# A hybrid attention, convolution, Fourier and linear-attention layer on one core: the second projection pass formed by seven half products a pair of tiles

## The reference

```python
hN = rms_norm(x, norm_g_l) * (1.0 + scale) + shift
p = hN @ w_in_l                       # 1024 -> 3616 columns
(qA, kA, vA, gA, bB, cB, hB, gB, uC, gC, qD, kD, vD, gD, aF, aB) = split_in(p)
yA = from_heads(attn_fn(q, k, v)) * silu(gA)      # window 8 x 16 plus 512 context keys
yB = short_conv(bB, cB, hB, conv_l) * silu(gB)    # bB * conv3(cB * hB)
yC = fourier_mix(uC) * silu(gC)                   # real part of a 2-D DFT, 4 groups of 64
yD = gla_mixer(...) * silu(gD)
y = concatenate([yA, yB, yC, yD]) @ w_out_l
return x + gate * y
```

## Time and profile before

| | |
|---|---|
| median of 3 runs | 2613.84 us (2611.82 to 2617.17) |
| the profiled execution | 2597.12 us, span 2595.4 us |
| TensorE busy | 2433.3 us, 94% of the span |
| VectorE, ScalarE, GpSimd busy | 1258.5, 931.3, 695.8 us |
| second projection pass | from about 944 to 1561 us |
| attention and scan | 1561 to 2168 us |

### The profile page before, as it was taken

The page is one execution under the profiler, slowest core; times in us unless marked ns, Lnnn a source line. Parts: engine busy times, 40 slices in busy tenths (PEclk is TensorE's granted clock), DMA queues, the critical chain, the costliest instruction groups (busy, mean ns, idle before and its releaser), DMA issues. The chain is left out here.

```text
span 2595.4 us, 52554 instructions
## 1 busy us (share of the span) xinstructions
PE 2433.3 (94%) x18684; PEld 1982.4 (76%) x18684; DVE 1258.5 (48%) x2614; ACT 931.3 (36%) x1954; POOL 695.8 (27%) x1014
## 2 busy tenths in 40 slices
PE   3899999999999969999999997999999995999999
PEld 1688888888888857888888876777777774888887
DVE  2534444344443434332333324667677665666665
ACT  1445454444545432111111114555556553111110
POOL 2232332323333220000000003433333333444442
PEclk8899999999999979999999998999999998999999
DMA  7655555656555452212222327877677787666663
GB/s 286 158 124 123 124 116 128 120 122 130 117 128 114 101 162 85 66 59 66 69 67 64 114 71 161 182 174 166 154 168 166 191 238 236 220 204 220 204 221 133
DMA packets 282000, 373.13 MB, mean 144 GB/s; under 512 B 52805, under 2 KB 211589, under 8 KB 280187
## 3 DMA queue, kind: packets, MB, share of 16 engines
q1 hardware_dynamic: 271660, 350.39, 52.7%
q10 hardware_dynamic: 9599, 19.75, 2.3%
q0 software_dynamic: 592, 0.99, 0.1%
HBM read 249.36 MB, written 121.66 MB: 143 GB/s over the span
## 5 line engine op out<-in xcount | busy, mean ns | idle before, releaser
L271 PE MATMUL p_ps_m<-p_w_hi,p_h_hi 128*128 128x512 f32 x1904 | 757.9, 398 | 17.0 <-DVE p_h_lo L1041 8.8
L273 PE MATMUL p_ps_m<-p_w_hi,p_h_lo 128*128 128x512 f32 x1904 | 745.5, 392 | 0.0
L272 PE MATMUL p_ps_m<-p_w_lo,p_h_hi 128*128 128x512 f32 x1904 | 744.5, 391 | 0.0
L271 PEld LDWEIGHTS p_ps_m<-p_w_hi,p_h_hi 128*128 128x128 f32 x1904 | 359.8, 189 | 94.5 <-issue 18.5
L273 PEld LDWEIGHTS p_ps_m<-p_w_hi,p_h_lo 128*128 128x128 f32 x1904 | 359.4, 189 | 77.6
L272 PEld LDWEIGHTS p_ps_m<-p_w_lo,p_h_hi 128*128 128x128 f32 x1904 | 359.9, 189 | 71.1
L1125 DVE TENSOR_TENSOR p_rows<-p_ps_m,p_silu_g 128x256 f32<-128x256 f32 x34 | 14.4, 425 | 319.8 <-ACT p_silu_g L869 319.8
L721 POOL TENSOR_TENSOR p_la<-p_la,p_cum 128x512 f32<-128x512 f32 x34 | 43.9, 1291 | 398.1 <-ACT p_cum L759 398.1
L1827 DVE COPY l_p_t<-a_ps_t 128x512 f32<-128x512 f32 (+1 forms) x136 | 91.5, 673 | 113.3 <-PE a_ps_t L1641 113.2
L703 POOL TENSOR_TENSOR q_hi_t<-q_hi,p_ones 128x128 fp32r<-128x128 f32 x2 | 0.9, 456 | 522.5 <-DMA q_lo<-s_qk_lo 522.5
L1677 PEld LDWEIGHTS a_ps_o<-a_v_win,l_p_t 128*64 128x64 f32 x2112 | 74.7, 139 | 61.9 <-issue 45.4
(11 more groups left out here) (291 smaller groups left out, 4559.5 us busy)
## 6 DMA issues: line engine op xcount, KB each, us to landing
s_scan<-b_w_raw SPq DMA_DIRECT2D x136, 128.0 KB, 2.4
a_scan<-s_scan SPq DMA_DIRECT2D x67, 258.0 KB, 6.3
a_kv<-s_kv SPq DMA_DIRECT2D x67, 256.0 KB, 6.3
a_v_win<-s_p SPq DMA_DIRECT2D x132, 128.0 KB
b_xr<-in_x_sample SPq DMA_DIRECT2D x32, 512.0 KB, 6.2
b_xt<-in_x_sample_t SPq DMA_DIRECT2D x32, 512.0 KB, 7.1
p_xt<-in_x_columns_t SPq DMA_DIRECT2D x32, 512.0 KB, 10.5
o_x<-in_x_sample SPq DMA_DIRECT2D x32, 512.0 KB, 4.7
```

What stands on the lines that cost most here:

```text
L271: pe.matmul(out, left_hi(k), right_hi(k), start=(k == 0), stop=False)
L272: pe.matmul(out, left_hi(k), right_lo(k), start=False, stop=False)
L273: last = pe.matmul(out, left_lo(k), right_hi(k), start=False, stop=(k == K8 - 1))
```

## The change

The second pass gets a function of its own, `column_stage`. Tiles go in pairs (17). The first two pairs (`PLAIN`) are made as before. In the others group 2 is still made for each tile, but groups 0 and 1 of both tiles, as a product of a 2 x 2 block matrix (tiles x depth halves) with a 2 x 2 block matrix (depth halves x column groups), are formed by Winograd's form of Strassen's scheme: seven half products of 12 matmuls (p1 to p7) in place of eight. For it sums of weights (`fold` on VectorE in the plain tiles, `fold_last` on GpSimd) and sums of x blocks (`sum_pair` on GpSimd, split by `high_sums` and VectorE) are made; the seven results are joined by ScalarE, VectorE and GpSimd through `part_a`, `part_b`, `part_c`, and GpSimd multiplies the gates (`mix_rows`). The rows of both tiles are sent at the end of a pair, the odd one first.

The space for this is taken from the early loads: only queries and keys are still loaded in the second pass. Bias table 0, context keys and their halves, context values, state and the order of the first queries move to the start of the attention stage, g and dft_whole (for the last Fourier rows) too. Fourier rows have four slots in place of three, the output stage has its own y_hi and y_lo, and waits for the convolution's taps before its first tile.

```diff
+def column_pairs(eng):
...
+def column_stage(nc, io, keep, early):
+
+    pieces = weight_pieces(PASS_BLOCKS[1])
+    pieces[:4] = [(None, 0, 0, 0, 0, 0)] * 2 + [(k, 4, GC, W_GRP, W_GRP, 0) for k in (0, 4)]
...
+            def send_rows(t, s, p):
...
+                else:
+                    sp.wait_ge(gates_done, t + 1)
+                    sp.wait_ge(mixed[s], p + 1)
+                gates = rows[s][:, 1:3, :].rearrange("t a c -> t (a c)")
...
+                else:
+                    columns = lambda a: a.rearrange("(a b) c -> b a c", b=GRID_W)[bass.ds(2 * t, 2)]
+                    sp.dma_start(columns(io["conv_u"][SKIP[0]:SKIP[0] + N_GRID, :]), rows[s][:, 0, :]).then_inc(rows_sent[s], 16)
+                    sp.dma_start(columns(io["gates_bc"][0:N_GRID, :]), gates).then_inc(rows_sent[s], 16)
...
+                for s in range(2):
+                    t = p * 2 + s
+                    if prompt(p):
+                        continue
+                    sp.wait_ge(lo_done if plain(p) else s_lo_done, t + 1)
+                    load_turned(t + 2, s, kind(t + 2))
+                    load_norm(t + 2, s, kind(t + 2))
...
+                    sp.wait_ge(s_lo_done, 2 * PAIRS)
+                    for to, name in (("q_hi", "qk_hi"), ("q_lo", "qk_lo")):
+                        sp.dma_start(early[to][:, :, :].bitcast(F32), io[name][0:2, :, queries].rearrange("p k t -> k p t")).then_inc(early_in, 16)
...
+                else:
+                    send_columns(p * 2, 0)
+                send_rows(p * 2 + 1, 1, p)
+                send_rows(p * 2, 0, p)
...
+            def fold_last(k):
+
+                for n, (a, b, op) in enumerate(((w_hi[:, K4 + k, 512:1024], w_lo[:, K4 + k, 512:1024], ALU.add), (part_c, w_hi[:, k, 512:1024], ALU.subtract),
+                                                (part_c, w_lo[:, k, 512:1024], ALU.subtract))):
...
+            def sum_pair(p):
+                pool.wait_ge(lo_done, p * 2 + 2)
+                a11, a12, a21, a22 = xt[0][:, 0:K4, :], xt[0][:, K4:K8, :], xt[1][:, 0:K4, :], xt[1][:, K4:K8, :]
+                pool.tensor_tensor(a22, a21, a22, ALU.add).then_inc(summed, 1)
+                pool.tensor_tensor(a21, a11, a21, ALU.subtract).then_inc(summed, 1)
+                pool.wait_ge(summed, p * 4 + 2)
+                pool.tensor_tensor(a11, a22, a11, ALU.subtract).then_inc(summed, 1)
+                pool.wait_ge(summed, p * 4 + 3)
+                pool.tensor_tensor(a12, a12, a11, ALU.subtract).then_inc(summed, 1)
+
+            def mix_rows(p, s, part, done):
+                pool.wait_ge(group_kept, p * 2 + 1 + s)
+                pool.wait_ge(done, p + 1)
+                pool.tensor_tensor(rows[s][:, 1, :], rows[s][:, 1, :], part[:, 0:W_GRP], ALU.mult)
+                pool.tensor_tensor(rows[s][:, 0, :], rows[s][:, 0, :], part[:, W_GRP:512], ALU.mult).then_inc(mixed[s], 1)
+
+            pool.wait_ge(t_lo_done, 3 * K4)
+            pool.wait_ge(plain_mm, 3 * 2 * PLAIN - 2)
+            for k in range(2):
+                fold_last(k)
+            for p in column_pairs(pool):
...
+                    continue
+                sum_pair(p)
+                if isinstance(p, int) and p == PLAIN:
+                    for k in range(2, K4):
+                        fold_last(k)
+                pool.wait_ge(u3_done, p + 1)
+                pool.wait_ge(a5_kept, p + 1)
+                pool.tensor_tensor(part_a, part_a, part_b, ALU.add).then_inc(u4_done, 1)
+                pool.tensor_tensor(part_b, part_c, part_b, ALU.add).then_inc(c22_done, 1)
+                mix_rows(p, 1, part_b, c22_done)
+                mix_rows(p, 0, part_a, c12_done)
...
+            def high_sums(p, s):
...
+            def keep_group(p, s, done):
+                act.wait_ge(rows_sent[s], p * 32 + 16)
+                act.activation(rows[s][:, 0, :], bank_b[s][:, 0:W_GRP], ACT.Copy)
+                act.activation(rows[s][:, 1, :], bank_b[s][:, W_GRP:512], ACT.Silu).then_inc(done, 1)
...
+            for t in range(2 * PLAIN):
...
+                act.wait_ge(plain_mm, plain_at(t, 0))
+                if t > 1:
+                    act.wait_ge(y_mm, t - 1)
+                act.activation(g_sb[s], plain_bank[s][0][:, 0:W_GRP], ACT.Copy)
+                act.wait_ge(rows_sent[s], p * 32 + 16)
+                act.activation(rows[s][:, 2, :], plain_bank[s][0][:, W_GRP:512], ACT.Silu).then_inc(plain_g, 1)
+                if t:
+                    act.wait_ge(plain_mm, 3 * t)
+                high(t + 1, 1 - s)
+                act.wait_ge(t_sums, 7 * t + 7)
+                for n, part in enumerate((part_a, part_b, part_c)):
+                    last = act.activation(t_hi[:, n, t, :], part, ACT.Copy)
+                last.then_inc(t_hi_done, 1)
+                if t:
...
+            for p in column_pairs(act):
+                if plain(p):
+                    continue
+                for s in range(2):
...
+                keep_group(p, 0, group_kept)
+                keep_columns(p * 2 - 1, 1, p - 1)
+                act.wait_ge(group_mm, p * 2 + 2)
+                keep_group(p, 1, group_kept)
+                if isinstance(p, int) and p == PLAIN:
+                    act.wait_ge(t_lo_done, 3 * K4)
+                act.wait_ge(mixed[0], p)
+                act.wait_ge(p1_mm, p + 1)
+                act.activation(part_a, bank_x[:, :], ACT.Copy).then_inc(a1_kept, 1)
+                act.wait_ge(c11_done, p + 1)
+                act.activation(rows[0][:, 2, :], rows[0][:, 2, :], ACT.Silu).then_inc(gates_done, 1)
+                act.wait_ge(mixed[1], p)
+                act.wait_ge(p5_mm, p + 1)
...
+                    act.wait_ge(p4_mm, p + 1)
+                    high(p * 2 + 3, 1)
+                act.wait_ge(c21_done, p + 1)
...
+            def half_product(out, left, right):
...
+                for k in range(K4):
+                    pe.matmul(out, left(0, k), right(0, k), start=(k == 0), stop=False)
+                    pe.matmul(out, left(0, k), right(1, k), start=False, stop=False)
+                    last = pe.matmul(out, left(1, k), right(0, k), start=False, stop=(k == K4 - 1))
+                return last
...
+                for s in range(2):
+                    pe.wait_ge(lo_done, p * 2 + 1 + s)
...
+                pe.wait_ge(a5_kept, p)
...
+                    pe.wait_ge(plain_rows, 2 * PLAIN - 1)
...
+                if begin:
...
+                pe.wait_ge(s_lo_done, p * 2 + 2)
...
+                    pe.wait_ge(plain_g, 2 * PLAIN)
+                half_product(bank_z[:, :], lambda part, k: sums[part][0][:, k, :], lambda part, k: turned[part][:, 1, k, :]).then_inc(p6_mm, 1)
+                pe.wait_ge(a1_kept, p + 1)
+                half_product(bank_x[:, :], lambda part, k: sums[part][1][:, K4 + k, :], lambda part, k: turned[part][:, 0, k, :]).then_inc(p5_mm, 1)
...
+                    first_step(p * 2, 0, g_done)
+                pe.wait_ge(c11_done, p + 1)
+                if begin:
...
+                half_product(bank_y[:, :], lambda part, k: sums[part][1][:, k, :], lambda part, k: w[part][:, k, 512:1024]).then_inc(p7_mm, 1)
+                pe.wait_ge(u2_done, p + 1)
+                half_product(bank_z[:, :], lambda part, k: sums[part][0][:, K4 + k, :], lambda part, k: w[part][:, K4 + k, 512:1024]).then_inc(p3_mm, 1)
...
+            def fold(k):
...
+                full = lambda half, g: (w_hi[:, half * K4 + k, g * 512:g * 512 + 512], w_lo[:, half * K4 + k, g * 512:g * 512 + 512])
+                steps = ((part_a, *full(0, 0), ALU.add), (part_b, *full(0, 1), ALU.add), (part_a, part_b, part_a, ALU.subtract), (part_b, *full(1, 1), ALU.add),
+                         (part_b, part_b, part_a, ALU.subtract), (part_c, *full(1, 0), ALU.add), (part_c, part_c, part_b, ALU.subtract))
+                for n, (out, a, b, op) in enumerate(steps):
+                    dve.wait_ge(t_sums, 7 * k + n)
+                    dve.tensor_tensor(out, a, b, op).then_inc(t_sums, 1)
...
+            for t in range(2 * PLAIN):
+                p, s = t // 2, t % 2
+                norm(t + 1, 1 - s, (t + 1) // 2)
+                fold(t)
+                low(t + 1, 1 - s)
+                fold_low(t)
+                dve.wait_ge(rows_sent[s], p * 32 + 16)
+                dve.wait_ge(plain_mm, plain_at(t, 1))
+                dve.wait_ge(plain_b, t + 1)
+                dve.tensor_tensor(rows[s][:, 1, :], plain_bank[s][1][:, 0:W_GRP], rows[s][:, 1, :], ALU.mult)
+                dve.tensor_tensor(rows[s][:, 0, :], plain_bank[s][1][:, W_GRP:512], rows[s][:, 0, :], ALU.mult).then_inc(plain_rows, 1)
...
+            for p in column_pairs(dve):
+                if plain(p):
+                    continue
+                for s in range(2):
+                    dve.wait_ge(s_hi_done, p * 2 + 1 + s)
+                    dve.tensor_tensor(s_lo[s][:, :, :], xt[s], s_hi[s][:, :, :], ALU.subtract).then_inc(s_lo_done, 1)
+                if not prompt(p):
```

(95 more changed lines are left out.)

437 lines of the change are left out of this document (352 added, 85 removed).

## The result

The change made the kernel slower: 2658.15 us median of 4 runs (2651.78 to 2662.26) against 2615.51 (2611.82 to 2620.28), ratio 1.016 with a 95% interval of 1.0132 to 1.0187. The forecast was 2663.

A forecast was written before the change was run, and what follows sets the result against it. TensorE's matmul count bounded the kernel; after the change, a loop through row writes was to set 36.0 us a pair. Stage +45, attention +5, Fourier slot -1 gave +49 on 2613.84: 2663, own range 2643 to 2683, wider range 2600 to 2690.

The forecast's parts named there:

- four two-engine writes in a row: Each pair's conv_u and gates_bc writes for both tiles queue on the same two DMA engines, taking 18.1 us.
- two loops that the prediction names: Second pass: x tile behind writes, 35.2 us before SBUF sharing; ScalarE's keep_group waiting for sent rows, nearly the same length.
- Rival (a): Row writes spread, or even and odd tiles overlap: pair 31.57 us, change -27, kernel 2587; chance 0.18.
- The pair: Steady pair of tiles in the second pass: T = 36.0 us, bounds 31.8 and 37.5, against 34.3 before.
- sharing of SBUF: VectorE and GpSimd slow each other on the x-tile loop: 0.8 us a pair (0 to 1.5).
- Rival (b): SBUF sharing and low clock fall fully on the pair's loop: T 37.5, 21 us more, 2684; chance 0.15.
- Start of the stage: Second pass's first tiles: tile 1 +4.0 us, tile 3 +7.4 and 1.8 of low clock; pair 2 starts +13.2.
- N(2): End of tile 6's norm in the third pair, forecast at 1085.8 us in the earlier trace's time.
- End of the stage: From the last pair's writes to the next stage +21.2 us: stage ends at 1606.0 against 1561.0, +45.
- Attention: Attention's first inputs load late: the stall before its first value product grows from 15.1 to about 20, +5 (1 to 10).
- the fourth Fourier slot: Late in the second pass it takes away ScalarE's wait for a sent slot: -1 us.
- Sum: Whole kernel: 45 + 5 - 1 = +49 us on the profiled 2597.12, carried over to the runs' median 2613.84: 2663.

The follow-up runs named there:

- spread_after: The changed kernel with each column-ordered write of rows sent as two writes of 64 rows, one per grid column: 2586.31 us against 2598.28 before the change, ratio 0.9957.
- folds_vector: The changed kernel with the last four weight sums made by VectorE instead of GpSimd: ratio 1.0168 to the kernel before.
- late_only: The changed kernel with its second pass made by the old function, undoing the seven half products: 2606.81 us against 2598.28 before the change, ratio 1.0030.
- odd_on_act: The changed kernel with the odd tile's two column-ordered writes issued by ScalarE on its own queue: ratio 1.0198 to the kernel before.

## Why the prediction was right, and where its terms were off

**The mechanism.** The four two-engine writes in a row, with the x tiles and ScalarE's keep_group behind them, set the pair. That is shown: with the same bytes on more engines the pair is TensorE's 31.57 us, with the writes some 8 us later it is 47.3, with half of them on another queue it stays. Of the two loops that the prediction names, none is shown to be the longer one: u3 (1253.14) follows on VectorE, busy without a gap since its x tile landed, and on product 7, whose last matmul begins at 1252.65. And the x tile waits on the two engines, not for SP: its load is issued at 1232.66, once s_lo is made (1232.48), when the fourth write's issue is already over (1231.44). Rival (a) failed at the premise that it stood on, four writes side by side; and its price was too good as well: spread_after, which has the pair that it assumed, stands at 0.9957 where it gave 2587 / 2613.84 = 0.990.

**The pair, 36.0 forecast, 35.38 measured.** From the end of norm (1245.38 + 2.14 = 1247.52) to the first row write (1259.15) are 11.6 us, where the loop had 10.95 and 0.8 for sharing of SBUF. From that issue to the next end of norm are 23.8, where it had 24.25. (Its 9.05 us for two writes are 9.10 by its own terms, 11.85 - 1.1 - 1.3 - 0.35.) Rival (b), 37.5, has no support: sharing cost about what was put. On the loop it is GpSimd's part_b, 2.15 in place of 1.29:

```profile
1255.15 2.15 POOL L1313 TENSOR_TENSOR p_work<-p_part_c,p_work 128x512 f32<-128x512 f32 x1
```

VectorE's low of the odd tile beside it takes 2.8 us, but nothing on the loop waits for it.

**Start of the stage.** Tile 1 was 3.9 us later (4.0 forecast), tile 3 began at 82.3 (83.5). The third pair began at 102.0 (102.5). Then the term that failed: the norm of tile 6, N(2) in the prediction, was to end at 132.4 and ended at 139.5. GpSimd's weight sums were counted by their own length, but not what they do to VectorE. The eight scalings of tile 6 took 7.18 us and those of tile 5 10.15, in place of 2.14. folds_vector shows the cause: with the sums on VectorE both take 2.14 or 2.15, and the norm of tile 6 ends at 133.0. The Trainium skill ("SBUF — State Buffer", SBUF: two separate sides) says that an operation of VectorE in a two-port mode, or with two SBUF inputs, and one of GpSimd hold the shared ports for the whole instruction and exclude each other; the trace agrees in the time, 10.15 / 8 = 1.27 us for each scaling, the length of one GpSimd sum. Which mode the scalings, with one input, run in no trace shows. The prediction had looked for such sharing only in operations with two SBUF inputs.

**End of the stage.** The last keep_group came at 629.6 (632.1 forecast): 13 steps of 35.38 gave back 8.1 us, the third pair had cost 7.1, and from the last norm to this keep_group were 30.3 us and not 31.7. From there to the next stage were 18.1 us (20.5). The stage ended 40.1 us later than before, 45 were forecast; that it is so near is in part luck, since two misses of some 7 us had nearly cancelled.

**Attention.** +7.5 to the first value product (22.8 after the start, 15.3 before), 5 forecast. After it 1.4 us came back, where the fourth Fourier slot was to give 1; late_only, with the same slot, loses 3.3 there in its trace, so such differences are not told from noise, and the slot's 1 us is not shown.

**Sum.** 40.1 + 7.5 - 1.4 = 46.2 in the traces, 42.6 by the medians, 49 forecast. Carrying the 49 over from the trace's 2597.12 to the runs' median was right as far as the traces tell: the 13 us that they differ by in the first pass are the chip's, with either kernel.

## What to carry to other kernels

Saving work on the bounding engine pays only while every loop beside it stays shorter; write down each loop through buffers and queues with its transfers in it, not the load of each engine. Results that are formed together leave together: transfers that were hidden one by one stand in a row, and their shape (how many engines one can use) is then worth more than their bytes. An operation moved to GpSimd was charged twice here, by its own length and by what it held up on VectorE.

## What was not expected of the hardware

- VectorE's short operations suffer most beside GpSimd's sums: the 128x128 scalings 1.27 us each for 0.27, the 128x128 subtraction of two SBUF tiles 1.37 for 0.28 (changed kernel, line 1544), the subtraction of 1024 elements only 1.74 for 1.23. The number of inputs is not what tells there; each short operation lasts about as long as one of GpSimd's.
- Splitting the column-ordered writes in two costs SP four more issues a pair, of some 0.6 us each, and brings the writes of a pair from 18 us to 6.
- Four such writes in a row hold the issuing queue itself: the fourth takes 5.25 us to issue, where the first takes 0.58. In odd_on_act, with two of them on each of two queues, SP's pair in the steady stretch takes 0.58 and 0.53, and in spread_after the eight take 0.6 each.
